# Low halves of weights written over the raw tiles, with the split of a unit two ahead in the middle of the running one

## The reference

```
h = h + mixer(rms_norm(h));  h = h + swiglu(rms_norm(h))            # first block, twice
x = x + gate * mixer(modulate(rmsnorm(x)));  x = x + gate * relu(modulate(rmsnorm(x)) @ w1)**2 @ w2
```

## Time and profile before

| | |
|---|---|
| median of 3 runs | 2984.96 us |
| span of the profiled execution | 2983.2 us |
| TensorE busy | 2888.3 us, 97% |
| VectorE busy | 2004.9 us, 67% |
| ScalarE busy | 1202.5 us, 40% |
| GpSimd busy | 349.9 us, 12% |
| mean granted TensorE clock | 0.992 |
| subtractions L1932 | 626, 739.2 us |
| high halves L1602 | 626, 620.6 us |

### The profile page before, as it was taken

How to read it: one execution, slowest core, us unless ns; L and a number is a source line. 1 busy time by engine, 2 the same in 40 slices (tenths; PEclk the granted TensorE clock), 3 DMA queues, 4 the chain that set the end, 5 groups by cost and what they waited for, 6 DMA issues and landing times.

```text
span 2983.2 us, 43523 instructions
## 1 busy us (share of the span) xinstructions
PE 2888.3 (97%) x18080; PEld 2524.0 (85%) x18080; DVE 2004.9 (67%) x3284; ACT 1202.5 (40%) x1993; POOL 349.9 (12%) x542
## 2 busy tenths in 40 slices
PE   7999999989999999999999999999999999998998
PEld 7999998889997778888866888888888888877898
DVE  7776887668655557777745677777777777554665
ACT  5444544554444444223314533223243222443543
POOL 0000001000022220000131100011010000243000
PEclk9999999999999999999999999999999999999999
DMA  7544675347655424555473255553535555465453
GB/s 241 168 159 152 216 229 190 120 161 234 204 125 81 72 64 147 157 167 169 132 190 107 80 168 163 169 165 124 170 120 164 168 163 169 117 96 86 142 184 128
DMA packets 362277, 451.85 MB, mean 151 GB/s; under 512 B 12656, under 2 KB 332432, under 8 KB 362080
## 3 DMA queue, kind: packets, MB, share of 16 engines
q1 hardware_dynamic: 326976, 329.83, 34.1%
q0 software_dynamic: 34944, 118.65, 16.9%
q10 hardware_dynamic: 160, 0.59, 0.1%
HBM read 438.60 MB, written 1.05 MB: 147 GB/s over the span
## 4 chain that ended last, share of the span: by engine, by line
PE 79%; DVE 12%; ACT 5%; DMA 2%; issue 1%; POOL 1%; DVEq 0%; SPq 0%; ACTq 0%
PE ps L1352 23%; PE ps L1354 23%; PE ps L1353 23%; DVE lo L1932 4%; PE ps L1530 1%; ACT hi L1602 1%; PE ps L1373 1%; PE ps L1517 1%; DVE NB L1963 1%; DMA NB<-in_na_rpb 1%; PE ps L1375 1%; PE ps L1374 1%; DVE MX L2008 1%; PE ps L1505 1%; DVE XN L1969 1%
## 5 line engine op out<-in xcount | busy, mean ns | idle before, releaser
L1352 PE MATMUL ps<-XN,hi 128*128 128x256 f32 (+1 forms) x3184 | 1048.8, 329 | 32.9 <-DVE XN L1949 9.9
L1353 PE MATMUL ps<-XN,hi 128*128 128x256 f32 (+1 forms) x3184 | 1029.9, 323 | 0.0
L1354 PE MATMUL ps<-XN,lo 128*128 128x256 f32 (+1 forms) x3184 | 1029.6, 323 | 0.0
L1932 DVE TENSOR_TENSOR lo<-raw,hi 128x1024 fp32r<-128x1024 f32 (+1 forms) x626 | 739.2, 1221 | 250.6 <-ACT hi L1602 245.4
L1602 ACT ACTIVATE hi<-raw 128x1024 fp32r<-128x1024 f32 (+1 forms) x626 | 620.6, 1040 | 443.5 <-PE ps L1354 440.7
L1352 PEld LDWEIGHTS ps<-XN,hi 128*128 128x128 f32 x3184 | 610.6, 192 | 106.6 <-issue 17.4
L1354 PEld LDWEIGHTS ps<-XN,lo 128*128 128x128 f32 x3184 | 610.8, 192 | 46.1
L1353 PEld LDWEIGHTS ps<-XN,hi 128*128 128x128 f32 x3184 | 611.2, 192 | 44.8
L2008 DVE CUSTOM_DVE_ANT_0 MX<-MW,C 128x1024 bf16<-128x1024 f32 x384 | 477.2, 1243 | 130.7 <-DMA MW<-in_mod_w 123.8
L1352 PE MATMUL ps<-H,hi 128*128 128x512 f32 (+1 forms) x1072 | 380.2, 355 | 0.0
L1353 PE MATMUL ps<-H,hi 128*128 128x512 f32 (+1 forms) x1072 | 379.7, 354 | 0.0
(11 more groups left out here) (255 smaller groups left out, 3194.8 us busy)
## 6 DMA issues: line engine op xcount, KB each, us to landing
raw<-in_mlp_w SPq DMA_DIRECT2D x128, 1024.0 KB, 5.3
MW<-in_mod_w POOLq DMA_DIRECT2D x192, 512.0 KB, 3.8
raw<-in_ffn_w_in SPq DMA_DIRECT2D x44, 1024.0 KB, 5.4
raw<-in_attn_w_in SPq DMA_DIRECT2D x36, 1024.0 KB, 4.9
raw<-in_na_wqkv SPq DMA_DIRECT2D x24, 1024.0 KB, 5.0
raw<-in_ffn_w_out SPq DMA_DIRECT2D x16, 1024.0 KB, 5.1
raw<-in_mlstm_w_in SPq DMA_DIRECT2D x12, 1024.0 KB, 5.1
raw<-in_cv_w SPq DMA_DIRECT2D x12, 1024.0 KB, 6.2
```

Source lines behind the costliest of these rows:

```text
L1352: e.matmul(out, whi, xhi, start=first, stop=False)
L1353: e.matmul(out, whi, xlo, start=False, stop=False)
L1354: i = e.matmul(out, wlo, xhi, start=False, stop=last)
L1932: e.tensor_tensor(lo[:, a:b], raw[:, a:b], hi[:, a:b].bitcast(F32), ALU.subtract).then_inc(*low.says(("lo", j, i), ("spent", j) if i else ...
```

## The change

The raw and the low tile of a unit share one buffer: the low part is written over the raw one. There are 4 such buffers and 3 for the high part, again 7 of 1 MB. A load of unit j waits for "used" of j - 4, and `take(j)` brings units up to j + 3. The split of unit j waits for its raw tile alone (VectorE) and for "used" of j - 3 (ScalarE, through the high buffer). Splits are now kept with their unit's number, and `splits(upto)` writes those up to it: `take(j)` those up to j + 1, and the middle of unit j the one of j + 2. The middle is behind the evacuation of tile 0 in `linear`, ahead of the end of the first part in `close`, half-way through the token tiles in `linear_tok`, and behind the first half in SwiGLU's out stage. In the stages whose units run together the split stands at the end of them, as before.

```diff
-RAW = 3
-HL = 2
+RAW = 4
+HL = 3
...
-    m.raw = [sb(f"raw{i}", [P, 2048]) for i in range(RAW)]
+    with ExitStack() as st:
+        m.raw = [sb(f"raw{i}", [P, 2048], F32, st) for i in range(RAW)]
+    m.lo = [sb(f"lo{i}", [P, 2048], F32R) for i in range(RAW)]
     m.hi = [sb(f"hi{i}", [P, 2048], F32R) for i in range(HL)]
-    m.lo = [sb(f"lo{i}", [P, 2048], F32R) for i in range(HL)]
...
-    def splits(self):
-        while self.late:
-            self.late.pop(0)()
+    def splits(self, upto):
+
+        while self.late and self.late[0][0] <= upto:
+            self.late.pop(0)[1]()
 
     def take(self, *unit):
-        self.splits()
         j = len(self.units)
+        self.splits(j + 1)
         self.units.append(unit)
         known = self.known
         if known is not None:
             while self.unit_next < len(known):
                 i = self.unit_next
-                if i > j and (i - j > HL or (i >= RAW and i - RAW not in self.known_raw)):
+                if i - j > HL:
                     break
                 self.bring(i)
                 if i == j:
-                    self.splits()
+                    self.splits(j)
                 self.unit_next += 1
...
@@ linear
                 evac(t, *banks[i])
+            if group[0] == 0:
+                self.splits(j + 2)
             if not (outer or quiet):
@@ close
                     self.do("rstd_part", s, 0, *sums[0], self.rs_user)
+                if (i, t) == (0, 0):
+                    self.splits(j + 2)
@@ linear_tok
             evac(t, b, u)
+            if t == ntt // 2 - 1:
+                self.splits(j + 2)
@@ norm_streams
-                    self.splits()
+                    self.splits(self.last_unit + 2)
@@ grow_wide
-            if c == 0 and self.late:
-                self.late.pop(0)()
+            if c == 0:
+                self.splits(units[0] + 2)
@@ swiglu
                     p.residual(c * 2 + t, S, None, *banks[t], True)
+                if t == 0:
+                    p.splits(j + 2)
@@ between, and the conformer
-    p.splits()
+    p.splits(p.last_unit + 2)
@@ load (SP)
         if j >= RAW:
-            w.wait_ge(("spent", j - RAW))
+            w.wait_ge(("used", j - RAW))
@@ split (VectorE)
-        raw, hi, lo = m.raw[j % RAW], m.hi[p.slot[j]], m.lo[p.slot[j]]
+        raw, lo, hi = m.raw[j % RAW], m.lo[j % RAW], m.hi[p.slot[j]]
         cuts = cuts_of(p, j)
-        before = p.split_before[j]
-        w.wait_ge(("raw", j), None if before is None else ("used", before))
+        w.wait_ge(("raw", j))
         for i in only or (0, 1):
             a, b = cuts[i:i + 2]
             w.wait_ge(("hi", j, i))
             e.tensor_tensor(lo[:, a:b], raw[:, a:b], hi[:, a:b].bitcast(F32), ALU.subtract).then_inc(
-                *low.says(("lo", j, i), ("spent", j) if i else None))
+                *low.says(("lo", j, i)))
```

More of the change, by code:

```diff
@@ L262, in __init__ @@
         self.pace, self.credit, self.parts = 0.0, 0.0, 0
-        self.made, self.known_raw = set(), set()
+        self.made = set()
         self.norms, self.rs_user, self.sa_user, self.sq_user = 0, None, None, [None, None]
@@ L288, in split @@
             self.do("split", j)
-            self.known_raw.add(j)
-        self.late.append(split)
-    def splits(self):
-        while self.late:
-            self.late.pop(0)()
+        self.late.append((j, split))
+    def splits(self, upto):
+        while self.late and self.late[0][0] <= upto:
+            self.late.pop(0)[1]()
     def take(self, *unit):
-        self.splits()
         j = len(self.units)
+        self.splits(j + 1)
         self.units.append(unit)
@@ L489, in first_norm @@
         self.do("split", 1)
-        self.known_raw.update((0, 1))
         self.sa_user = ("first_ones", KT - 1)
@@ L1274, in slot_of @@
     src, layer, k0, kt, c0, cols = p.units[j]
-    h = p.slot.get(j, 0)
-    return tuple(a[h][:, 0:kt * cols].rearrange("p (k n) -> p k n", k=kt) for a in (m.hi, m.lo))
+    halves = m.hi[p.slot.get(j, 0)], m.lo[j % RAW]
+    return tuple(a[:, 0:kt * cols].rearrange("p (k n) -> p k n", k=kt) for a in halves)
 def raw_of(m, p, j):
```

## The result

The changed kernel takes 3039.91 us (median of 4 runs, 3036.76 to 3040.64) against 2984.73 us: ratio 1.0182, 95% interval 1.017 to 1.0194. It is 55 us slower. The prediction said 2989.8 us with a range to 3000. One execution of one later kernel (experiment 6) ran at a granted clock of 0.687 and took 3868 us; it is left out of that kernel's time.

What follows compares the result with a forecast made beforehand. TensorE, busy 97% of the span, was taken as the bound, with about 95 us idle. Costs of 25.4 less gains of 20.6 gave net +4.8 on 2983.2, 2988.0 us profiled, 2989.8 as runs' median; range 2974 to 3000.

Steps and rivals of the forecast that it cites:

- start, C behind load 4: At the start, the conditions' loads go behind load 4, so C lands later and TensorE's unit 3 waits: +3.7 us.
- low halves: waits that go: TensorE's eleven stalls for low halves all go, as the split stands half a unit earlier: -12.7 us.
- conformer: The high half no longer waits for TensorE, so the sum TensorE waits for comes sooner: -1.35 us.
- last neighbourhood attention, exponent: The subtraction no longer stands right before the scores' exponent L2211, four places: -6.6 us, between 0 and -9.
- norm boundaries, 256 columns: A split between the last unit's two residuals delays the norm at five boundaries: +8.0 us, between 0 and +12.
- dilated attention, L2094: A subtraction comes before the copy of the transposed probabilities, VectorE having no hole: +4.8 us, between 0 and +9.6.
- neighbourhood attention, softmax waits: Subtractions beside the scores and ahead of the context scores' maximum, first and last layer: +8.9 us, between 0 and +21.
- mLSTM in units: As many splits between the VectorE and ScalarE chain's links, only at other links: 0, between -5 and +5 us.
- norm boundaries, 512 columns: Stages of 512 columns and closing units: TensorE waits for nothing of theirs, so 0.
- Rival C: Low halves' waits stay, late by engine queues or raw tiles, so 10.8 us don't come back: 3000.6 us, chance 0.07.
- Rival B: In the mLSTM, four heads' hand-overs each get a subtraction with no catching up: +9.4 us, 2999.2 us, chance 0.20.
- rival A: At norms and attention the costs don't reach TensorE, as VectorE works in slack: -9.9 us, 2975.1 us, chance 0.24.

Runs made afterwards that it cites:

- experiment 6: The changed kernel with the splits of the dilated attention's, first neighbourhood attention's and short convolution's in units back at the unit's start: 3018.87 us.
- experiment 2: The changed kernel without the middle split in the last unit ahead of a norm (quiet linear units, close, SwiGLU's last out unit): 3011.81 us.
- experiment 8: Also called the base: the changed kernel with no middle split and the conditions' loads ahead of load 4, new buffers kept: 2986.56 us.
- experiment 9: The kernel of experiment 8 with the middle split put back only in the last units ahead of a norm: 3015.85 us.
- experiment 3: The changed kernel with the middle split of SwiGLU's out stage ahead of the condition and tile 0's residual instead of behind them: 3026.99 us.
- experiment 5: The changed kernel with unit 4's load issued behind the conditions' loads (one unit fewer brought ahead for units 0 and 1): 3028.37 us.
- experiment 11: The kernel of experiment 8 with the middle split put back only in the mLSTM's in units: 2996.01 us.

## Why the prediction was wrong

Its terms against what the matmuls show, in us of waits (without the clock, the measured column adds up to 39.4, where the table by stage has 39.3):

| step | predicted | measured |
|---|---|---|
| start, C behind load 4 | +3.7 | +4.3 |
| low halves: waits that go | -12.7 | -11.9 |
| low halves: new waits | 0 | +8.3 |
| conformer | -1.35 | -1.5 |
| last neighbourhood attention, exponent | -6.6 | -6.9 |
| norm boundaries, 256 columns | +8.0 | +10.0 |
| dilated attention, L2094 | +4.8 | +5.2 |
| neighbourhood attention, softmax waits | +8.9 | +7.5 |
| mLSTM in units | 0 | +6.1 |
| norm boundaries, 512 columns | 0 | +12.9 |
| short convolution, YH | 0 | +5.4 |
| TensorE's clock | not priced | +15.9 |

Every term that was worked out from a row of its own place came out within 2.0 us. The sum failed at what was set to 0: by the sentence "Stages of 512 columns, the closing units and the feed-forward units: TensorE waits for nothing of theirs", by the one on the mLSTM, and, for the clock, by the opening one that "only about 95 us of TensorE's idle time, and nothing of the rest, can be changed by moving splits". The zero did hold for the buffers behind the start and for the MLPs' units that are not closing ones. In waits it failed in three ways, told below, and the clock comes on top.

Of the terms that came out, the norm boundaries' was right in size by luck in part. At the five boundaries of 256 columns the prediction had 1.33 or 2.0 us each; they measure 1.6, 1.9, 1.6, 1.1 and 3.9. Of the last, ahead of MLP 3, 2.36 us is the middle split's own (the matmul at 2838.26, which doesn't wait in experiment 2), and 1.1 comes without any middle split, in experiment 8 as well. And the wait that grew is not the norm's, which was to be the sign, but that of the sum ahead of it. The dilated attention's term held although its premise did not: from 76 to 101 us VectorE is not without a hole, it stands 1.7 us for ScalarE ahead of 82.13 and again ahead of 92.02.

First, the closing units. For 256 columns the prediction had seen that the split of the unit after next comes between two residuals. It didn't ask the same of 512 columns. There too, ScalarE's squares, GpSimd's sums of 1.3 us each and VectorE's residuals each wait for the one before, and what TensorE waits for is the end of that chain. Experiments 2 and 9 show it from both sides.

Second, the queue. A split moved to the middle of a unit was weighed against the residuals, not against the conditions, which stand in the same queue and wait for a DMA. This makes most of the new waits for low halves (+8.3, put at 0) and the one for YH (+5.4, put at 0). Rival C came nearest ("The low halves' waits stay, since ScalarE's and VectorE's queues and not the buffers made them late"), but was priced as old waits that stay; the old ones went and new ones came. Experiment 3 shows for the wait of 2.5 us that the order of split, condition and residual decides it; the one of 3.25 us can go without that.

Third, the mLSTM. That the number of splits between the chain's links is the same and they only sit at other links was put at 0; it gave 6.1 us of waits. At three links 2.3 to 2.8 us came, at three more 1.6 to 1.7, and 1.1 to 2.6 us went at four. Rival B had the place and the direction, with 9.4 us. Alone on the base the stage's splits cost 9.5 us, but that the numbers meet is luck: rival B counted four subtractions with no catching up and no clock, and the trace has 3.3 us of waits and 4.6 of pace.

The clock is the largest single miss. TensorE's busy time, which the prediction took for fixed, grew by 15.9 us. The trace of before showed that it could: the mean was 0.96 in the mLSTM stage, where TensorE waits often. In the changed kernel a wait is paid 1.4 times on the mean: 39.3 us of waits came with 15.9 us of slower matmuls, 0.4 us for each. The price isn't fixed: against before, it is 0.2 us for each in the executions of experiments 3 and 5 (27.3 and 35.0 us of waits with 5.6 and 6.6 of pace) and 0.8 in that of experiment 2 (19.2 with 15.3).

Right were: the subtraction in place (1220 ns against 1221), the loads (5.1 us to landing, no wait for a raw tile), ScalarE's wait in the conformer, and that rival A is wrong: the costs do reach TensorE. So was the reading of GpSimd's long bias adds. Two subtractions and two adds that overlap, in the kernel before:

```profile
2628.67 2.90 DVE L1932 TENSOR_TENSOR lo<-raw,hi 128x1024 fp32r<-128x1024 f32 x2 [0.62 <-ACT hi L1602]
2629.06 3.09 POOL L2409 TENSOR_TENSOR NB<-NB,cst 128x256 f32<-128x256 f32 x2 [7.70 <-DMA NB<-in_na_rpb]
```

Alone they take 2.36 us and 1.44. All adds over 1 us, 11 before and 3 after, began while a subtraction was in work; adds that began first and then met one took 726 to 745 ns. TensorE's wait behind this place fell by 2.2 us; the prediction had 1.9 with the adds' delay and 1.3 without. VectorE's waits for the add fell from 3.6 us to 1.4 over the span. The Trainium skill, SBUF — State Buffer, section "SBUF: two separate sides", has the two engines block each other at a shared port pair. The traces agree: in the changed kernel the subtractions have left most of these adds alone, and the three long ones (up to 1721 ns) are those that they still meet.

Left open: why the untouched mLSTM stage is 4.5 us faster in pace in experiments 3 and 5 than in the changed kernel with the same waits. Only one execution of each was traced, so it isn't known whether this goes with the kernel or changes from one execution to the next.

## What to carry to other kernels

Ask of every place at which moved work can land what stands in the same queue there, not only what waited there before: a zero in such a sum needs a row of its own. Work in the middle of a unit is good where an engine is idle until its scores come, and bad ahead of anything whose last link TensorE waits for; so place it by stage, not by one rule. And price each new wait of TensorE with a clock part: 0.4 us per us in the changed kernel, 0.2 to 0.8 in the others.

## What the runs showed of the hardware

- A subtraction of 128x1024 whose output is its own input takes 1220 ns, as one into another buffer does (1221).
- A GpSimd add of 128x256 that begins while such a subtraction is in work ends 585 to 598 ns behind the subtraction's end, in each of 14 cases in the two traces; it then takes 1122 to 1721 ns, and 726 to 745 when it began first. The subtraction that comes behind such an add takes up to 1767 ns.
- The spread of a kernel's times does not follow from its waits: the kernel before spans 2 to 6 us over its runs, the changed one, with the most waits, 4 us over four, experiment 11 15 us over ten, and experiment 3 13 us over four.
- Untouched stages differ by up to 5 us between two traced executions: the last neighbourhood attention is 5.0 us faster in experiment 11 than in its base with the same code, 2.8 of it waits and 2.3 pace. The cause is not known.
